# Two decoder layers on one core: expert groups of 64 and of 32 places in turn, and part of an output projection among the last heads

## The chip, the cores and the metric

The kernel runs on one core of one Trainium2 chip. The metric is the device time of that core in microseconds (us). Before the change the median of 3 runs is 1320.36 us (1319.8 to 1320.96).

## The reference, cut to what matters

256 tokens of 1024 channels pass through two layers, all in float32. The change touches the mixer of layer 0 and the mixture of experts (MoE) of both layers.

```python
# layer 0: h = x @ w_in; a convolution branch u (width 31, then LayerNorm, silu)
# beside 8 attention heads o; then one output projection of both
mix = concat([u, o], axis=-1) @ w_out + b_out          # (256, 1024) @ (1024, 1024)
x = layer_norm(ALPHA * x + mix)
# MoE of each layer: 64 experts of hidden width 256, 6 chosen for each token
def expert_step(acc, p):
    wg, wu, wd, g = p
    hid = silu(t @ wg) * (t @ wu)                      # wg, wu: (1024, 256)
    return acc + (hid @ wd) * g[:, None], None         # wd: (256, 1024)
shared = (silu(t @ sh_w_gate) * (t @ sh_w_up)) @ sh_w_down
x = layer_norm(ALPHA * x + routed + shared)
```

Layer 1 has 16 heads of another kind of attention in place of layer 0's mixer. The sum over the experts doesn't depend on the order in which they are taken, but for rounding.

## The kernel before

Five engines run programs of their own and meet at semaphores: SyncE (SP) issues nearly all large DMAs, TensorE (PE) multiplies, ScalarE (ACT) and VectorE (DVE) take results out of PSUM, GpSimd (POOL) does small work. PSUM has 8 banks; `plan_banks` lists the use of each bank in the order of the program, and an engine waits on `bank_free` or `bank_full` of a bank with the count that this list gives.

**Experts.** The 64 experts of a layer are worked off in 16 groups of 4 (`GE`). One group's weights are 12 pieces of 1 MB (gate, up and down of 4 experts) and fill 12 of the 13 units of `ring`. There is no second set: a unit is filled for the next group as soon as this group's last matmul on it is done. SP does this in `refill`, which for each piece waits on the PSUM bank of the matmuls that last use the unit (`last_use_of_weights`), and then issues the DMA. It does so in one of two orders:

```python
IN_ORDER = [(j, w) for j in range(GE) for w in range(2)] + [(j, 2) for j in range(GE)]
BY_KIND = [(j, w) for w in range(3) for j in range(GE)]
```

`j` is the expert of the group, `w` is 0 for gate, 1 for up, 2 for down. `IN_ORDER` thus brings gate and up of expert 0, then of expert 1, and so on, and all downs at the end; `BY_KIND` all gates, then all ups, then all downs. The order is that of the group that lets the units go, not of the group that the weights are for.

A group has one of two forms. The *wide* form has 64 places for the tokens of each expert. It works on pairs of experts: gate and up of experts 0 and 1 together (`gate_up(lp, 0)`, line 1016, one bank), then of experts 2 and 3, then the down products by pairs (line 1039), and last it scatters the rows back onto the tokens (line 1119). The *narrow* form has 32 places for each, so that the 4 experts stand side by side: all gates (line 1141), all ups (the same line, another bank), all downs (line 1169), scatter (line 1178). Each group also gathers the tokens of the group after it, into `xg` for a wide one (line 987) or `xn` for a narrow one (`pairs`, line 1051).

The experts stand sorted by the number of their tokens from the second half of group 0 on, the fullest first. `KINDS` says which form the groups have: 5 wide ones (`first`, three of the kind `wide`, and `turn`, which gathers for a narrow one), then 11 narrow ones. The wide groups are written out, the narrow ones are a loop of two groups a turn on PE, ACT and DVE. Between `turn` and the first narrow group stands `shared_down`, the down product of the shared expert (line 979).

**Layer 0's mixer.** The program of the heads is `attention`: scores of head h+1, then `between(h)`, then the product with V for a pair of heads (bank key `ot`, line 696), then the transposition of the probabilities (`pt`, line 705). In layer 0 `between` is `conv`, which puts parts of the convolution on PE (line 804), and DVE has its parts of the convolution (line 1564) between the softmax of the heads. After the heads PE transposes the convolution's result to rows (`urow`, line 817), DVE and ACT do LayerNorm and silu on it, and meanwhile PE begins the output projection `mix` with the attention half (its `ks` are 2 and 3, line 830): 4 results of 128x512, for each of them 4 matmuls. Then come the transpositions `uT` (line 845) and the convolution half of `mix` (`ks` 0 and 1). An fp32 matmul stands in the trace as two records, so that those 16 matmuls are x32.

## Time and profile before

| what | value |
| --- | --- |
| median of 3 runs | 1320.36 us |
| profiled execution | 1321.53 us |
| its span, first to last instruction | 1319.8 us |
| mean granted TensorE clock | 0.928 of full |
| busy: PE, DVE, ACT, POOL | 1075.3, 416.3, 259.1, 79.6 us |
| DMA | 447.53 MB, mean 339 GB/s |

The span is 1.7 us shorter than the execution's own time. The 40 slices of the page (33 us each) show five stretches: the mixer of layer 0 up to about 165 us, its experts up to about 650 us at 390 to 423 GB/s with one slice of 362, the mixer of layer 1 up to about 805 us, its experts up to about 1305 us in the same manner, and a short end. The page's chain of work that ended last has DMA and PE as its two large shares.

### The profile page before, as it was taken

To read this page: it belongs to the slowest core of one execution; us is meant where nothing else is said; L and a number is where in the kernel's file an instruction comes from. 1 tells how busy PE (TensorE), PEld (TensorE's weight loads), DVE (VectorE), ACT (ScalarE), POOL (GpSimd) and SP (SyncE) were. 2 spreads that over 40 slices of the span, in tenths; PEclk is the share of its full clock that TensorE was granted. 3 is DMA by queue.
4 is the path that set the end of the run, shared out by engine and by line. 5 is a ranking of instruction groups with operands and counts; after the bars stand their busy time and mean duration, and the time that the engine had idled before them with its cause. 6 is when DMAs were issued, how large, how long until landed. Compare 5 with 4: busy or idle time off the path is not lost.

```text
span 1319.8 us, 19934 instructions
## 1 busy us (share of the span) xinstructions
PE 1075.3 (81%) x7616; PEld 644.1 (49%) x7616; DVE 416.3 (32%) x993; ACT 259.1 (20%) x619; POOL 79.6 (6%) x106
## 2 busy tenths in 40 slices
PE   7977999999777776676499999999997777676663
PEld 4764744544444443343288866445444444333341
DVE  2584633332212222211322235333322122222113
ACT  3562322121111111111022233222211111111110
POOL 1343100000000000000141000000000000000000
PEclk9998999999988888888799999999999888888887
DMA  8172479999899999999971263699999999999994
GB/s 346 58 286 96 176 283 390 416 416 418 362 421 422 423 422 421 422 422 421 363 243 37 92 255 128 263 393 415 418 416 372 421 422 422 422 422 422 422 422 173
DMA packets 78946, 447.53 MB, mean 339 GB/s; under 512 B 7579, under 2 KB 20311, under 8 KB 29734
## 3 DMA queue, kind: packets, MB, share of 16 engines
q1 hardware_dynamic: 75840, 439.25, 81.6%
q0 software_dynamic: 1904, 6.46, 1.4%
q10 hardware_dynamic: 1142, 1.01, 0.2%
q8 instruction: 39, 0.64, 0.2%
q14 instruction: 21, 0.17, 0.0%
HBM read 445.61 MB, written 1.05 MB: 338 GB/s over the span
## 4 chain that ended last, share of the span: by engine, by line
PE 56%; DMA 35%; issue 3%; DVE 2%; SPq 2%; ACT 1%; ACTq 0%; DVEq 0%; POOL 0%; POOLq 0%
DMA ring<-in_l_exp_w_up 34%; PE bank L1016 11%; PE bank L1141 10%; PE bank L1039 5%; PE bank L866 4%; PE bank L830 4%; PE bank L987 3%; PE bank L1119 3%; PE bank L932 2%; PE bank L869 2%; PE bank L743 2%; SPq L583 2%; DMA mixT<-in_l_conv_w 1%; PE bank L979 1%; DVE side L1564 1%
## 5 line engine op out<-in xcount | busy, mean ns | idle before, releaser
L1141 PE MATMUL bank<-ring,big 128*32 128x256 f32 x2816 | 216.1, 475 | 147.5 <-DMA ring<-in_l_exp_w_up 110.2
L1141 PEld LDWEIGHTS bank<-ring,big 128*32 128x32 f32 x2816 | 120.1, 135 | 238.2 <-issue 195.0
L1016 PE MATMUL bank<-ring,big 128*64 128x512 f32 x640 | 142.2, 596 | 0.0
L1905 DVE TENSOR_TENSOR big<-big,bank 128x256 f32<-128x256 f32 x22 | 9.3, 421 | 331.8 <-PE bank L1141 331.8
L1926 DVE TENSOR_TENSOR mixT<-mixT,bank 128x512 f32<-128x512 f32 x128 | 84.1, 683 | 29.7 <-PE bank L1119 16.7
L1169 PE MATMUL bank<-ring,big 128*32 128x512 f32 x704 | 80.5, 595 | 8.6 <-DMA ring<-in_l_exp_w_down 7.3
L1411 ACT ACTIVATE ys_high<-bank,gcol 128x512 fp32r<-128x512 f32 x84 | 57.7, 687 | 147.6 <-PE bank L1169 88.2
L1016 PEld LDWEIGHTS bank<-ring,big 128*64 128x64 f32 x640 | 44.0, 137 | 82.1 <-issue 80.5
L1051 PE MATMUL bank<-pick,xs_high 128*128 128x128 f32 x352 | 82.9, 280 | 0.0
L2035 POOL TENSOR_TENSOR rstd<-rstd,half 128x1 f32<-128x1 f32 x10 | 13.3, 1333 | 1133.1 <-DVE rstd L1499 1133.1
L1051 PE MATMUL bank<-pick,xs_low 128*128 128x128 f32 x352 | 81.0, 275 | 0.0
L1039 PE MATMUL bank<-ring,big 128*64 128x512 f32 x320 | 73.1, 598 | 0.0
L1051 PEld LDWEIGHTS bank<-pick,xs_high 128*128 128x128 f32 x352 | 67.6, 192 | 9.9 <-issue 9.9
L1178 PE MATMUL bank<-ys_high,hot 128*128 128x512 f32 x88 | 42.5, 482 | 32.6 <-DVE ys_low L1913 21.8
L1051 PEld LDWEIGHTS bank<-pick,xs_low 128*128 128x128 f32 x352 | 67.5, 192 | 0.0
L866 PE MATMUL bank<-xT,ring 128*128 128x256 f32 (+1 forms) x320 | 59.8, 349 | 3.8 <-issue 3.8
L1398 ACT ACTIVATE big<-bank 128x256 f32<-128x256 f32 x44 | 16.9, 384 | 232.5 <-PE bank L1051 232.5
L1913 DVE SCALAR_TENSOR_TENSOR ys_low<-bank,gcol,ys_high 128x512 fp32r<-128x512 f32 x44 | 33.0, 751 | 83.4 <-ACT ys_high L1411 83.4
L830 PE MATMUL bank<-ring,mixT 128*128 128x512 f32 x128 | 57.5, 604 | 0.8 <-ACT mixT L1351 0.8
L866 PEld LDWEIGHTS bank<-xT,ring 128*128 128x128 f32 x320 | 53.5, 202 | 9.3 <-issue 4.3
L1178 PEld LDWEIGHTS bank<-ys_high,hot 128*128 128x128 f32 x88 | 16.4, 186 | 76.7 <-issue 58.9
L1866 DVE SCALAR_TENSOR_TENSOR ys_low<-bank,gcol,ys_high 128x512 fp32r<-128x512 f32 x40 | 30.0, 750 | 64.5 <-ACT ys_high L1411 64.5
(285 smaller groups left out, 1362.0 us busy)
## 6 DMA issues: line engine op xcount, KB each, us to landing
ring<-in_l_exp_w_gate SPq DMA_DIRECT2D x128, 1024.0 KB, 16.8
ring<-in_l_exp_w_up SPq DMA_DIRECT2D x128, 1024.0 KB, 16.9
ring<-in_l_exp_w_down SPq DMA_DIRECT2D x120, 1024.0 KB, 18.4
ring<-in_l_w_in SPq DMA_DIRECT2D x12, 1024.0 KB, 12.2
ring<-in_l_w_out SPq DMA_DIRECT2D x8, 1024.0 KB, 5.8
ring<-in_l_exp_w_down SPq DMA_DIRECT2D x16, 512.0 KB, 15.7
ring<-in_l_w_in SPq DMA_DIRECT2D x4, 1440.0 KB, 14.9
par<-in_l_ln_g POOLq DMA_DIRECT2D x4, 512.0 KB, 6.4
```

What stands on the lines that cost most here:

```text
L830: ins = mm(ps[:], mixT[:, 2 * k + j, P * tb:P * tb + P], w[:, j, HALF * h:HALF * h + HALF], start=start, stop=stop)
L866: ins = mm(ps[:, T * s + t.start:T * s + t.stop], w[:, c, P * s:P * s + P], xT[:, c, t], start=(c == 0), stop=(c == C - 1))
L987: ins = mm(ps[:, 0:GSLOT], xs[k][:, tb, P * c:P * c + P], pick[:, tb, :], start=(tb + k == 0), stop=(tb + k == 2))
L1016: ins = mm(ps[SLOTS * q:SLOTS * q + SLOTS, :], xg[:, c, SLOTS * j:SLOTS * j + SLOTS], both[:, c], start=(c == 0), stop=(c == C - 1))
L1039: ins = mm(ps[SLOTS * q:SLOTS * q + SLOTS, :], hidT[pr][:, m, SLOTS * q:SLOTS * q + SLOTS], wt[:, m, HALF * h:HALF * h + HALF], start=(m = ...
L1051: ins = mm(ps[:, n * s:n * s + n], xs[k][:, tb, P * (2 * c + s):P * (2 * c + s) + P], pick[:, tb, 0:n], start=(tb + k == 0), stop=(tb + k ...
L1119: ins = mm(ps[:], hot[:, pr, P * tb:P * tb + P], ys[k][:, pr, HALF * h:HALF * h + HALF], start=(pr + k == 0), stop=(pr + k == 2))
L1141: ins = mm(ps[r, 0:HID], xn[:, c, r], loop_weights(L, j, w)[:, c, :], start=(c == 0), stop=(c == C - 1))
L1169: ins = mm(ps[r, :], hidT[0][:, m, r], loop_weights(L, j, 2)[:, m, HALF * h:HALF * h + HALF], start=(m == 0), stop=(m == 1))
L1178: ins = mm(ps[:], hot[:, 0, P * tb:P * tb + P], ys[k][:, 0, HALF * h:HALF * h + HALF], start=(k == 0), stop=(k == 1))
L1411: fn(ys[0][:, pr, HALF * h:HALF * h + HALF], ps[:], ACT.Copy, scale=gcol[:, pr:pr + 1])\
L1926: lp.done(v.tensor_tensor(part, part, ps[:], ALU.add), ("scatter", n))
```

## The change

It has four parts.

1. The groups have the forms wide, wide, narrow, wide, narrow, wide, narrow, wide, narrow, and then 7 narrow ones: still 5 wide and 11 narrow. `PLACE` keeps the sorted experts with the form that they had: the wide groups take places 0 to 4 of the sorted list, as before. Each single group is now written out on every engine, SP too; the loop has 6 of the last 7 narrow groups. A narrow group ahead of a wide one gathers for the wide form.
2. `shared_down` stands after the ninth group in place of the fifth.
3. In layer 0's mixer PE does 4 of the attention half's 16 matmuls (first two results, `ks` 2) in `between(8)` and `between(9)`, behind the last head, and the next 4 (the same results, `ks` 3) ahead of the transpositions `urow`; the other 8 stay behind them. The banks change with it: `urow` has 0 and 1, the first two results have 6 and 7. The convolution half for the first 128 tokens waits for their `uT` alone.
4. On DVE the last piece of the convolution comes after the last head's probabilities, not before them.

```diff
-KINDS = (("first", 1), ("wide", 3), ("turn", 1), ("narrow", 11))
+KINDS = (("first", "wide", "wide", 1), ("turn0", "wide", "narrow", 1),
+         ("back0", "narrow", "wide", 1), ("turn1", "wide", "narrow", 1),
+         ("back1", "narrow", "wide", 1), ("turn2", "wide", "narrow", 1),
+         ("back2", "narrow", "wide", 1), ("turn3", "wide", "narrow", 1),
+         ("single", "narrow", "narrow", 1), ("narrow", "narrow", "narrow", 7))
+PLACE = (0, 1, 5, 2, 6, 3, 7, 4, 8, 9, 10, 11, 12, 13, 14, 15)
+ALONE = [k for k, _, _, n in KINDS if n == 1]
+LATE = TIMES["narrow"]
...
     for tb in range(TB):
-        u.add(("urow", tb), 6 + tb)
+        u.add(("urow", tb), tb)
     for tb in range(TB):
         for h in range(2):
-            u.add(("mix", 0, tb, h), 2 * tb + h)
+            u.add(("mix", 0, tb, h), [6, 7, 2, 3][2 * tb + h])
...
+    def next_place(self):
+        if self.r is None and self.kind != "narrow":
+            return GE * PLACE[BEGIN[self.kind] + 1]
+        return self.groups(GE, GE)
```

On SyncE:

```diff
-                lp = ExpertLoop(L, "wide", banks, S, bank)
-                with sp.Fori(0, dict(KINDS)["wide"]) as i:
-                    lp.i = i
-                    refill(lp, in_place(lp.groups(GE, GE)))
...
+                for kind in ALONE[1:]:
+                    lp = ExpertLoop(L, kind, banks, S, bank, i=0)
+                    refill(lp, in_place(lp.next_place()))
```

On TensorE, in layer 0's mixer (`attention`, `conv`, and behind the heads):

```diff
-                    if h < heads:
+                    if h < heads or L == 0:
                         between(h)
...
+                if h >= H0:
+                    if h == H0:
+                        for g in range(2):
+                            bank_moved(pe, ("ot", 0, g))
+                    mix(0, 0, h - H0, (2,), last=False)
+                    return
...
+            for g in range(2, H0 // 2):
+                bank_moved(pe, ("ot", 0, g))
+            for h in range(2):
+                mix(0, 0, h, (3,), first=False, last=False)
+            bank_moved(pe, "convT")
+            pe.wait_ge(S("conv_dve"), 1)
+            pe.wait_ge(S("conv_pool"), TAPS)
...
-            for g in range(H0 // 2):
-                bank_moved(pe, ("ot", 0, g))
-            for tb in range(TB):
-                for h in range(2):
-                    mix(0, tb, h, (2, 3), last=False)
+            for h in range(2):
+                mix(0, 1, h, (2, 3), last=False)
...
-                if L == 0:
-                    for tb in range(TB):
+                for tb in range(TB):
+                    if L == 0:
                         bank_moved(pe, ("uT", tb))
-                for tb in range(TB):
                     for h in range(2):
```

On TensorE, in the experts:

```diff
-                        pairs(lp, (0, 1))
+                        gathers(lp, (0, 1, 2, 3))
...
-                        pairs(lp, (2, 3))
+                        gathers(lp, (4, 5, 6, 7))
...
-                for i in range(dict(KINDS)["wide"]):
-                    wide(ExpertLoop(L, "wide", banks, S, bank, i=i))
-                wide(ExpertLoop(L, "turn", banks, S, bank, i=0))
+                for kind in ALONE[1:]:
+                    (wide if FORM[kind] == "wide" else narrow)(ExpertLoop(L, kind, banks, S, bank, i=0))
                 shared_down()
```

On VectorE, in the heads of layer 0:

```diff
-                    if between:
+                    if between and h < heads:
                         between(h)
...
+                    if between and h == heads:
+                        between(h)
```

ACT and DVE get the same choice between `gathered` and `pair` in both forms (`tokens`).

TensorE behind the last heads of layer 0, before. L705 transposes probabilities, L696 is the product with V, L817 is `urow`, L830 is `mix`, with the bank of each:

```order
L705 MATMUL bank3<-ident,att 128x128 [waits probs,bank_free3]
L705 MATMUL bank3<-ident,att 128x128 x2
L696 MATMUL bank4<-att,V 64x256 [waits bank_free3,bank_free2,bank_free4]
L696 MATMUL bank4<-att,V 64x256
L696 MATMUL bank4<-att,V 64x128 x2
L817 MATMUL bank6<-ident,side 128x128 [waits conv_pool,bank_free6,conv_dve,bank_free5]
L817 MATMUL bank6<-ident,side 128x128 x3
L817 MATMUL bank7<-ident,side 128x128 [waits bank_free7]
L817 MATMUL bank7<-ident,side 128x128 x3
L830 MATMUL bank0<-ring,mixT 128x512 [waits bank_free4,bank_free0,unit_full10]
L830 MATMUL bank0<-ring,mixT 128x512
L830 MATMUL bank0<-ring,mixT 128x512 [waits unit_full11]
```

At this place nothing of the projection stands ahead of `urow`. The same place now, where L816 is `mix`, L721 the transposition, L712 the product with V:

```order
L816 MATMUL bank6<-ring,mixT 128x512 [waits bank_free6,unit_full10,bank_free4]
L816 MATMUL bank6<-ring,mixT 128x512
L721 MATMUL bank3<-ident,att 128x128 [waits probs,bank_free3]
L721 MATMUL bank3<-ident,att 128x128 x2
L816 MATMUL bank7<-ring,mixT 128x512 [waits unit_full10,bank_free7]
L816 MATMUL bank7<-ring,mixT 128x512
L712 MATMUL bank4<-att,V 64x256 [waits bank_free3,bank_free2,bank_free4]
L712 MATMUL bank4<-att,V 64x256
L712 MATMUL bank4<-att,V 64x128 x2
L816 MATMUL bank6<-ring,mixT 128x512 [waits unit_full11,bank_free4]
L816 MATMUL bank6<-ring,mixT 128x512
L816 MATMUL bank7<-ring,mixT 128x512 [waits unit_full11]
```

Four matmuls of `mix`, into banks 6 and 7, have moved around the last transposition of probabilities, and the next four follow the last product with V (the fourth of them is cut off here), with `urow` behind them.

TensorE at the start of the third group of layer 0, before: the gate factors are transposed (L1090), then come the two products of gate and up of a wide group (L1016), each of 16 matmuls on the weights of two experts, and the transposition of the hidden rows (L1027):

```order
L1090 MATMUL bank2<-ident,att 128x128 [waits bank_free2,moe0_pick]
L1090 MATMUL bank2<-ident,att 128x128 x3
L1016 MATMUL bank0<-ring,big 64x512 [waits unit_full6,bank_free0,unit_full7,bank_free5,unit_full9,bank_free4,unit_full10,bank_free1]
L1016 MATMUL bank0<-ring,big 64x512 x15
L1016 MATMUL bank1<-ring,big 64x512 [waits unit_full3,unit_full1,unit_full4,unit_full0,bank_free1]
L1016 MATMUL bank1<-ring,big 64x512 x15
L1027 MATMUL bank0<-ident,big 128x128 [waits bank_free0]
L1027 MATMUL bank0<-ident,big 128x128
```

These wait for the gates and ups of two experts each. The same place now: the end of the second group's scatter (L1141), gate factors transposed (L1151), then all gates and all ups of a narrow group (L1163), and the gathering for the wide group after it (L1008):

```order
L1141 MATMUL bank7<-ys_high_51,hot_53 128x512
L1141 MATMUL bank7<-ys_low_52,hot_53 128x512
L1151 MATMUL bank0<-ident,att 128x128 [waits bank_free0,moe0_pick]
L1151 MATMUL bank0<-ident,att 128x128
L1163 MATMUL bank0<-ring,big 32x256 [waits unit_full9,unit_full6,unit_full0,bank_free0,unit_full3,bank_free5,bank_free4]
L1163 MATMUL bank0<-ring,big 32x256 x31
L1163 MATMUL bank1<-ring,big 32x256 [waits unit_full1,unit_full10,unit_full4,unit_full7,bank_free1]
L1163 MATMUL bank1<-ring,big 32x256 x31
L1008 MATMUL bank4<-pick_54,xs_high_49 128x256 [waits bank_free4,moe0_pick]
```

The third group's first product waits for the gates of 4 experts, and its second for the ups. In the fourth group the wide form's rows stand as before.

## Rows read from the trace of the kernel before

**Rows 1.** The page's chain that ended last, by line
```profile
DMA ring<-in_l_exp_w_up 34%; PE bank L1016 11%; PE bank L1141 10%; PE bank L1039 5%; PE bank L866 4%; PE bank L830 4%; PE bank L987 3%; PE bank L1119 3%; PE bank L932 2%; PE bank L869 2%; PE bank L743 2%; SPq L583 2%; DMA mixT<-in_l_conv_w 1%; PE bank L979 1%; DVE side L1564 1%
```

**Rows 2.** Windows: stretch, its length, busy us (instructions) by engine, PEclk, DMA share, GB/s
```profile
265.00:295.00 30.00, 30.00 (x153) 14.29 (x152) 9.36 (x18) 6.46 (x16) 0.00 (x0) 1.00 1.00 416
372.00:402.00 30.00, 20.75 (x208) 12.02 (x204) 6.30 (x12) 3.38 (x8) 0.00 (x0) 0.89 1.02 423
```

**Rows 3.** Timeline, SP: start, us, and what, each group's first weight DMA
```profile
212.34 0.35 SPq L583 DMA_DIRECT2D ring<-in_l_exp_w_gate  x1
...
242.54 0.34 SPq L583 DMA_DIRECT2D ring<-in_l_exp_w_gate  x1
...
302.92 0.34 SPq L583 DMA_DIRECT2D ring<-in_l_exp_w_gate  x1
...
337.02 3.19 SPq L583 DMA_DIRECT2D ring<-in_l_exp_w_gate  x4
...
872.97 0.35 SPq L583 DMA_DIRECT2D ring<-in_l_exp_w_gate  x1
...
997.66 2.03 SPq L583 DMA_DIRECT2D ring<-in_l_exp_w_gate  x4
```

**Rows 4.** Timeline, PE, narrow groups of layer 0: ups, gates, ups, ups
```profile
361.03 6.01 PE L1141 MATMUL bank<-ring,big 128*32 128x256 f32 x64 [4.50 <-DMA ring<-in_l_exp_w_up]
...
380.89 3.66 PE L1141 MATMUL bank<-ring,big 128*32 128x256 f32 x64 [1.63 <-DMA ring<-in_l_exp_w_gate]
390.83 6.46 PE L1141 MATMUL bank<-ring,big 128*32 128x256 f32 x64 [6.28 <-DMA ring<-in_l_exp_w_up]
...
420.63 5.23 PE L1141 MATMUL bank<-ring,big 128*32 128x256 f32 x64 [6.28 <-DMA ring<-in_l_exp_w_up]
```

**Rows 5.** Windows of 1 us around two first DMAs, columns as in Rows 2
```profile
212.00:213.00 1.00, 1.00 (x8) 0.42 (x6) 0.31 (x1) 0.38 (x1) 0.00 (x0) 1.00 0.04 16
...
336.00:337.00 1.00, 1.00 (x24) 0.76 (x20) 0.00 (x0) 0.12 (x1) 0.00 (x0) 1.00 0.00 0
```

**Rows 6.** Timeline, PE, second group: both gate and up products
```profile
205.07 13.96 PE L1016 MATMUL bank<-ring,big 128*64 128x512 f32 x64
```

**Rows 7.** Timeline behind layer 0's last heads, all engines
```profile
104.98 3.08 DVE L1564 SCALAR_TENSOR_TENSOR side<-side,cols 128x256 f32<-128x256 f32 x4
105.07 0.19 ACT L1249 ACTIVATION_READ_ACCUMULATOR att<-att,mx 128x1 f32 x1
...
105.20 0.52 PE L705 MATMUL bank<-ident,att 128*128 128x128 f32 x3
...
108.86 0.52 PE L705 MATMUL bank<-ident,att 128*128 128x128 f32 x3 [3.14 <-DVE att L1537]
...
110.05 1.55 PE L696 MATMUL bank<-att,V 128*64 128x256 f32 x8 [0.67 <-ACT att L1254]
...
111.64 0.38 ACT L1259 ACTIVATE mixT<-bank 128x256 f32<-128x256 f32 x1 [1.73 <-PE bank L696]
...
112.44 1.97 PE L817 MATMUL bank<-ident,side 128*128 128x128 f32 x8 [0.84 <-ACT side L1345]
...
114.20 15.13 PE L830 MATMUL bank<-ring,mixT 128*128 128x512 f32 x32
...
118.84 0.63 ACT L1348 ACTIVATE side<-side 128x512 f32<-128x512 f32 x1 [1.88 <-DVE side L1662]
...
129.16 1.04 PE L845 MATMUL bank<-ident,side 128*128 128x128 f32 x8
...
129.80 1.08 ACT L1351 ACTIVATE mixT<-bank 128x512 f32<-128x512 f32 x2 [10.33 <-PE bank L845]
...
130.99 4.53 PE L830 MATMUL bank<-ring,mixT 128*128 128x512 f32 x10 [0.79 <-ACT mixT L1351]
```

**Rows 8.** Windows of 2 us, PE alone: stretch, length, busy us, PEclk, DMA share, GB/s
```profile
104.00:106.00 2.00, 1.58 (x13) 1.00 0.30 45
...
112.00:114.00 2.00, 1.56 (x8) 0.50 0.98 322
```

More of the change, by code:

```diff
@@ L233, in __init__ @@
         self.tag = f"{'moe' if r is None else 'more'}{L}"
-        self.slots = NSLOT if kind == "narrow" else SLOTS
+        self.form, self.after = FORM[kind], AFTER[kind]
     def here(self, per, more):
@@ L788, in prog_tensor, with mix @@
                         bank_moved(pe, (name, tb, g))
+            def mix(L, tb, h, ks, first=True, last=True):
+                key = ("mix", L, tb, h)
+                ps = bank_open(pe, key) if first else bank[banks.at[key][0]]
+                for k in ks:
+                    unit_wait(pe, (f"out{L}", k))
+                    w = by_pair(unit((f"out{L}", k)))
+                    for j in range(2):
+                        start, stop = first and (k, j) == (ks[0], 0), last and (k, j) == (ks[-1], 1)
+                        ins = mm(ps[:], mixT[:, 2 * k + j, P * tb:P * tb + P],
+                                 w[:, j, HALF * h:HALF * h + HALF], start=start, stop=stop)
+                if last:
+                    bank_made(ins, key)
             def conv(h):
@@ L1412, in high, with tokens @@
                         .then_inc(lp.own("high"), 1)
+                def tokens(lp, c):
+                    if lp.after == "wide":
+                        gathered(lp.read, lp.done, ("gather", c))
+                    elif c % 4 == 0:
+                        pair(lp, c // 2)
                 def wide(lp):
@@ L1847, in wide @@
                 def wide(lp):
-                    after = "narrow" if lp.kind == "turn" else "wide"
                     if lp.kind == "first":
@@ L1949, in prog_vector @@
                 more = dve.value_load(rounds[0:1, 0:1], min_val=0, max_val=MAXR - 1)
[L1950 to L1952 removed]
+                for kind in ALONE[1:]:
+                    (wide if FORM[kind] == "wide" else narrow)(ExpertLoop(L, kind, banks, S, bank, i=0))
                 for tb in range(TB):
```

154 lines of the change are left out of this document (69 added, 85 removed).

## The prediction, made before the changed kernel ran

> **What bounds the kernel now.** I read first the page's chain by line, to see who carries the end [rows 1]: DMA of expert weights has 34%, and next to it stand PE lines of the wide groups (1016, 1039) and of the mixers (866, 830). So there are two regimes, and the windows by stage separate them [rows 2]. Among the wide groups PE is busy 30.00 of 30 us; among the narrow ones 20.75 of 30, and the DMA share is full in both, 416 and 423 GB/s. The experts are thus near a tie in the wide form and bound by DMA in the narrow one. How near is read from SP's first weight DMA of each group [rows 3]: 242.54 - 212.34 = 30.20 us for a wide group. For a narrow group the start of the ups repeats after 390.83 - 361.03 = 29.80 and 420.63 - 390.83 = 29.80 us [rows 4]; So 12 pieces take 29.80 us, 2.483 us a piece. That is what the weights need, whatever PE does.
>
> The rest is where DMA stands still inside the experts. In the window 212 to 213 it moves 16 GB/s, in 336 to 337 nothing [rows 5]: each time the ring is full and the first unit not yet let go. The second place is the change of form. From 302.92 to 337.02 are 34.10 us, 4.30 over 29.80 [rows 3]: the last wide group's 30.2 us and `shared_down` lie ahead of the first narrow gates.
>
> In the mixer I read the timeline behind the last heads [rows 7]: PE has nothing from 105.72 to 108.86, then works at half clock, and from 114.20 on is the bound with the projection until the transpositions `uT` at 129.16.
>
> **The experts, step by step.** Group 0 and group 1 stay wide, so group 2's first DMA still comes at the 212.34 of the trace, less what the mixer gives. To the first DMA of group 6 (337.02) the kernel takes 124.68 us for four groups, and 4 x 29.80 = 119.20 would do: 5.48 us to be had. In layer 1 it is 997.66 - 872.97 = 124.69, so 5.49 [rows 3]. The later groups are at 29.8 already. Whether the new order gets all of it depends on each group letting its first unit go within 29.80 us of its own weights' first issue, I. Two steps:
>
> Wide behind narrow. The narrow group refills by kind, so the wide group's first product (experts 0 and 1) needs the sixth piece. From issue to use there is a lag: 361.03 - 337.02 = 24.01 us for eight pieces, which take 19.87, so 4.14 [rows 3, 4]. Start: I + 4.14 + 6 x 2.483 = I + 19.04. PE has waited then, and is cold. The product takes 13.96 / 2 = 6.98 warm [rows 6]; the cold start costs 6.46 - 3.66 = 2.80 at most and 5.23 - 3.66 = 1.57 at least, by the narrow ups that also follow a wait for DMA [rows 4]. End I + 28.8, and SP issues 0.3 later (205.07 + 6.98 = 212.05 against 212.34 [rows 3, 6]): I + 29.1. It is 0.7 us in time, 1.9 with the small penalty. This is the tightest place of the change, three times a layer.
>
> Narrow behind wide. The wide group then ends its 30.2 us at I + 19.04 + 30.20 + 2.80 = I + 52.0, that is 22.2 after the narrow weights' first issue; the gates (seventh piece, at 4.14 + 17.38 = 21.5) are there. Gates 3.66 [rows 4], so the first unit goes at 26.2: 3.6 us in time. The four other products of that group have the wide gather's eight pieces beside them, about 1 us of waits for banks 0 and 1; PE reaches the next wide group some 6 us before its sixth piece, which hides it.
>
> The moved `shared_down` costs 6.9 us of PE (16 records; its slot is in the 34.10) and now stands where PE is idle 9 us of 30 [rows 2]. The next gates end at about 24 after issue, inside 29.8. Cost 0; without the cover it would be its 6.9 a layer. The written-out code adds instructions to every engine, no work to any: as many wide and narrow groups as before. The wide groups, written out already, run with PE 30.00 of 30 busy [rows 2], so I cost it at 0.
>
> Sum of the experts: 5.48 + 5.49 = 11.0 us.
>
> **The mixer, step by step** [rows 7]. Before, the last transposition waits for DVE (3.14 us), which does its 3.08 us of convolution first. Now the probabilities start when ACT has the exponentials, 105.26, and are there by 106.1 (the 0.8 between 108.06 and 108.86). PE goes on at 105.72 with two matmuls of `mix` at 0.86 (4 records at 13.8 / 32 = 0.43, warm): 107.44. Transposition to 107.96; two more matmuls beside ACT's copy of it: 109.7. Product with V, 1.55 at the low clock, some 0.8 warm: 110.6 with the waits at either end. ACT's copy of it, 0.38: 111.0. Four matmuls, 3.44: 114.45. Then `urow`; the convolution is in time: DVE ends at about 106.2 + 3.1 = 109.3, POOL before. `urow` takes 1.04 warm (the eight of 129.16), then eight matmuls, 6.88: 122.4. The silu of the second half ends 119.47 - 112.44 = 7.03 after `urow` starts, at 121.5: 0.9 in time. So `uT` starts at 122.4 in place of 129.16, 6.8 us. The first convolution half no longer waits for ACT's second copy: 1.08 / 2 = 0.54.
>
> Clock: 1.00 at 104 to 106, 0.50 at 112 to 114 behind the idle 3 us [rows 8]. Full is 2.4 GHz and 0.50 is 1.2 GHz. Now PE has no such gap. If it fell all the same, product, `urow` and the first matmuls would be as slow as now, 0.7 + 0.9 + 0.6 = 2.2 us less. Ends of this part: 5.1 and 7.4; I take 7.2, near the warm one, since what lowered the clock is filled. What follows (LayerNorm, router, group 0) keeps its distances, so the whole comes earlier by it.
>
> **Sum.** 11.0 + 7.2 = 18.2 us. The profiled execution of 1321.53 becomes 1303.3; it lies 1.2 above the median, and from 1320.36 the forecast is 1302.2.
>
> **Against it.** In the narrow stage the clock is down when PE comes back from DMA: 64 records take 6.01, 6.46 and 5.23 us instead of 3.66 [rows 4]. The Trainium skill, TensorE: Matmul & The Clock Gate, section "HAM oscillation — how this bites in real kernels", says that a kernel whose matmul pieces each follow a wait for DMA pays for the cold clock at every piece. The trace agrees for these rows; it shows too that the penalty ends inside the piece. The change puts the wide product behind such a wait. That is the rival on the other side.
>
> **Rivals.** (a) Cold wide groups: the first wide product runs at 1.2 GHz to its end, 13.96 instead of 9.8. It ends at I + 33.0, the next DMA comes at 33.3, 3.5 late; six times 21 us. 18.2 - 21 leaves the kernel at 1323, slower. It decides once the penalty passes 3.5 us. Against it: no ups row costs over 2.80. 4%. (b) The tight place is missed a little, 0.5 to 1 us each, or the first narrow gates come late: 3 to 6 us of the gain go, 1305.2 to 1308.2. For it: only 0.7 us of slack. 14%. (c) The mixer gives little, because PE's inserted matmuls hold the last head back or LayerNorm becomes the wait: 0 to 3 us, 1306.4 to 1309.4. Against it: the slack worked out above. 5%. (d) The DMA stream doesn't close up, since something I don't see holds SP (it now loads the experts' numbers in straight code): only the mixer's 7.2, 1313.2. 4%. (e) Both parts give nothing, the order only moves the waits: 1320, 3%. The forecast, 1300.5 to 1304.8, has 70%.
>
> **How the numbers follow.** A difference of 0.2% (2.6 us) is what a measurement here can tell. Faster: 70 + 14 + 5 + 4 = 93%. Same: 3%. Slower: 4%. The range 1300.0 to 1308.0 takes the forecast, (b) nearly whole and a third of (c).
>
> **What would show it.** SP's first weight DMAs from group 2 to group 6 stand 29.8 apart, with no window under 400 GB/s between 215 and 630 us (less the 7); `uT` at about 122; the wide L1037 product behind a wait for DMA, under 10 us for its first half, PE idle in the wide groups and not DMA. A penalty over 3.5 us, gaps of SP over 30 us, or `uT` later than 124 would prove a step wrong.

## The result, and the profile after

The changed kernel takes 1303.57 us (median of 4 runs, 1301.92 to 1303.92), the kernel before on the same chip 1320.66 us (1319.8 to 1322.14, 4 runs). The ratio is 0.9857, with an interval of 0.9839 to 0.9876: 1.4% faster, 17.1 us by the medians. The forecast was 1302.2 in 1300.0 to 1308.0.

The profiled execution of the changed kernel took 1301.92 us with a span of 1300.2, at a mean clock of 0.931. It is the fastest of its four, and the profiled execution before was above its median, so the two profiles differ by 19.6 us where the medians differ by 17.1. Landmarks on PE cut both spans into the same stretches; each is the start of a named product, and each distance is taken inside one profile:

| from, to | before | after | gain | forecast |
| --- | --- | --- | --- | --- |
| start to group 1's first product, layer 0 | 205.07 | 197.61 | 7.46 | 7.2 |
| to the last group's ups, layer 0 | 425.11 | 420.19 | 4.92 | 5.48 |
| to the first transposition of layer 1 | 24.61 | 24.48 | 0.13 | 0 |
| to layer 1's first projection product | 5.94 | 2.68 | 3.26 | 0 |
| to group 1's first product, layer 1 | 204.96 | 204.79 | 0.17 | 0 |
| to the last group's ups, layer 1 | 424.13 | 420.34 | 3.79 | 5.49 |
| to the end | 29.95 | 30.07 | -0.12 | 0 |

The page's chain for the kernel after, by engine and by line, to be set beside [rows 1]:

```profile
PE 52%; DMA 39%; issue 3%; DVE 2%; SPq 2%; ACT 1%; ACTq 0%; DVEq 0%; POOL 0%; POOLq 0%
DMA ring<-in_l_exp_w_up 33%; PE bank L1037 12%; PE bank L1163 10%; DMA ring<-in_l_exp_w_gate 5%; PE bank L888 5%; PE bank L816 4%; PE bank L1060 3%; PE bank L953 2%; PE bank L891 2%; PE bank L759 2%; PE bank L1141 2%; SPq L604 2%; PE bank L1008 1%; PE bank L1072 1%; DMA mixT<-in_l_conv_w 1%
```

DMA now has 39% of the chain (35% before), of which `ring<-in_l_exp_w_up` has 33%, about as before, and the gates have a share of their own (5%): the waits for weights have spread. PE is still the larger half (56% before, 52% now).

The windows of the kernel after, one of 30 us for each of four groups in turn and the ones behind (columns as in [rows 2]):

```profile
216.00:246.00 30.00, 28.32 (x262) 18.02 (x260) 11.61 (x22) 6.87 (x15) 0.00 (x0) 1.00 1.01 420
246.00:276.00 30.00, 24.27 (x110) 10.05 (x112) 5.54 (x11) 4.02 (x11) 0.00 (x0) 0.89 1.02 422
276.00:306.00 30.00, 27.67 (x255) 17.70 (x252) 11.89 (x22) 5.91 (x13) 0.00 (x0) 1.00 1.01 421
306.00:336.00 30.00, 23.25 (x103) 9.23 (x101) 3.61 (x8) 4.02 (x11) 0.00 (x0) 0.83 1.01 420
...
449.00:479.00 30.00, 21.59 (x208) 11.87 (x208) 6.30 (x12) 3.38 (x8) 0.00 (x0) 0.83 1.02 422
```

Where PE had 30.00 of 30 us in wide groups it now has idle time in every window, and DMA has none: 420 to 422 GB/s in each. Of the two hollow spots of [rows 5] the one at the change of form is gone. The one behind group 1's first product stays, since the change doesn't touch that group, and both kernels pay for it; it is the first window below. The other three are the same point in the turns, 3 us around each first DMA that a wide group lets go:

```profile
204.00:207.00 3.00, 3.00 (x16) 1.01 (x14) 0.42 (x1) 0.38 (x1) 0.00 (x0) 1.00 0.37 87
...
262.00:265.00 3.00, 3.00 (x17) 1.08 (x15) 0.42 (x1) 0.38 (x1) 0.00 (x0) 1.00 1.02 423
...
322.00:325.00 3.00, 3.00 (x16) 1.09 (x14) 0.42 (x1) 0.38 (x1) 0.00 (x0) 1.00 1.04 431
...
381.00:384.00 3.00, 3.00 (x18) 1.09 (x16) 0.42 (x1) 0.38 (x1) 0.00 (x0) 1.00 1.04 434
```

SP's first weight DMA of groups in the timeline after, answering to [rows 3]:

```profile
204.89 0.36 SPq L604 DMA_DIRECT2D ring<-in_l_exp_w_gate  x1
...
262.77 0.34 SPq L604 DMA_DIRECT2D ring<-in_l_exp_w_gate  x1
...
289.77 1.89 SPq L604 DMA_DIRECT2D ring<-in_l_exp_w_gate  x4
...
323.29 0.34 SPq L604 DMA_DIRECT2D ring<-in_l_exp_w_gate  x1
...
382.11 0.34 SPq L604 DMA_DIRECT2D ring<-in_l_exp_w_gate  x1
...
412.08 1.90 SPq L604 DMA_DIRECT2D ring<-in_l_exp_w_gate  x4
```

A stream with no hole would have these at 204.89 plus multiples of 29.80: 264.49, 294.29, 324.09, 383.69, 413.49 for the ones shown. Each issue is ahead of its due time, by 1.7, 4.5, 0.8, 1.6 and 1.4 us. The first, third and fourth are let go by wide groups, for which the prediction worked out 0.7 to 1.9; the second by a narrow group, for which it had 3.6. The last is that of the ninth group, which starts late itself (below).

PE in the same stretch: a narrow group's gates and ups, the wide pair that begins behind a wait for DMA, and the ninth group's gates and ups:

```profile
228.06 7.11 PE L1163 MATMUL bank<-ring,big 128*32 128x256 f32 x128 [0.72 <-issue]
...
253.46 16.00 PE L1037 MATMUL bank<-ring,big 128*64 128x512 f32 x64 [5.51 <-DMA ring<-in_l_exp_w_up]
...
406.52 8.80 PE L1163 MATMUL bank<-ring,big 128*32 128x256 f32 x128 [1.99 <-DMA ring<-in_l_exp_w_gate]
```

The wide pair starts at 253.46, where I + 19.04 from the due issue 234.69 gives 253.73 (I is the issue of a group's own first weights, as in the prediction). It takes 16.00 us instead of 13.96 [rows 6]; the two others (at 313.06 and 372.67, so 59.60 and 59.61 apart, twice 29.80) show 16.92 and 16.1. The granted clock is 0.50 in the window of 251 to 257, 0.95 in 257 to 263 and 1.00 behind it. So the cold start costs 2.0 to 3.0 us a pair.

Behind layer 0's heads, PE in the timeline after, answering to [rows 7]:

```profile
105.35 0.52 PE L721 MATMUL bank<-ident,att 128*128 128x128 f32 x3
...
105.70 1.88 PE L816 MATMUL bank<-ring,mixT 128*128 128x512 f32 x4
...
107.42 0.49 PE L721 MATMUL bank<-ident,att 128*128 128x128 f32 x3
...
107.75 1.88 PE L816 MATMUL bank<-ring,mixT 128*128 128x512 f32 x4
...
109.56 0.87 PE L712 MATMUL bank<-att,V 128*64 128x256 f32 x8
...
110.96 3.67 PE L816 MATMUL bank<-ring,mixT 128*128 128x512 f32 x8 [0.53 <-ACT mixT L1280]
...
114.47 1.04 PE L858 MATMUL bank<-ident,side 128*128 128x128 f32 x8
...
115.35 7.03 PE L816 MATMUL bank<-ring,mixT 128*128 128x512 f32 x16
...
123.50 14.00 PE L816 MATMUL bank<-ring,mixT 128*128 128x512 f32 x32 [0.25 <-ACT mixT L1372]
```

The window after that answers to [rows 8]:

```profile
112.00:114.00 2.00, 2.00 (x6) 1.00 0.92 279
```

No wait is over 0.8 us, and the window of 112 to 114 has the full clock (2.4 GHz) where [rows 8] had half of it. `uT` follows at 122.22. Counted from the last transposition but one, it comes after 16.87 us instead of 23.96: 7.09 us, free of what differs ahead of it. The convolution half of `mix` then starts 1.28 us after `uT` instead of 1.83, another 0.55.

### The profile page after: what moved, and what is told of

Read it like the earlier page. It is cut to its first block, busy times and chain, and to the rows that moved or that the text cites. A ratio compares the mean times of both kernels' runs of the same rounds, so it can differ in the third digit from the quotient of the medians.

```text
span 1300.2 us, 19603 instructions
## 1 busy us (share of the span) xinstructions
PE 1069.3 (82%) x7616; PEld 643.1 (49%) x7616; DVE 417.1 (32%) x993; ACT 259.7 (20%) x619; POOL 79.9 (6%) x106
## 4 chain that ended last, share of the span: by engine, by line
PE 52%; DMA 39%; issue 3%; DVE 2%; SPq 2%; ACT 1%; ACTq 0%; DVEq 0%; POOL 0%; POOLq 0%
DMA ring<-in_l_exp_w_up 33%; PE bank L1037 12%; PE bank L1163 10%; DMA ring<-in_l_exp_w_gate 5%; PE bank L888 5%; PE bank L816 4%; PE bank L1060 3%; PE bank L953 2%; PE bank L891 2%; PE bank L759 2%; PE bank L1141 2%; SPq L604 2%; PE bank L1008 1%; PE bank L1072 1%; DMA mixT<-in_l_conv_w 1%
## 5 line engine op out<-in xcount | busy, mean ns | idle before, releaser
L1163 PE MATMUL bank<-ring,big 128*32 128x256 f32 x2816 | 191.6, 435 | 99.9 <-DMA ring<-in_l_exp_w_up 70.5
L1163 PEld LDWEIGHTS bank<-ring,big 128*32 128x32 f32 x2816 | 114.3, 124 | 171.8 <-issue 131.0
L1037 PE MATMUL bank<-ring,big 128*64 128x512 f32 x640 | 156.2, 643 | 37.4 <-DMA ring<-in_l_exp_w_up 37.4
L1037 PEld LDWEIGHTS bank<-ring,big 128*64 128x64 f32 x640 | 50.0, 148 | 127.9 <-issue 126.3
L1191 PE MATMUL bank<-ring,big 128*32 128x512 f32 x704 | 85.3, 625 | 12.5 <-DMA ring<-in_l_exp_w_down 11.5
L1950 DVE TENSOR_TENSOR mixT<-mixT,bank 128x512 f32<-128x512 f32 x128 | 84.6, 683 | 29.2 <-PE bank L1141 16.9
L1929 DVE TENSOR_TENSOR big<-big,bank 128x256 f32<-128x256 f32 x22 | 9.3, 421 | 255.7 <-PE bank L1163 255.7
L1060 PE MATMUL bank<-ring,big 128*64 128x512 f32 x320 | 73.1, 598 | 0.0
L1882 DVE TENSOR_TENSOR big<-big,bank 128x256 f32<-128x256 f32 x20 | 8.4, 421 | 162.8 <-ACT big L1424 162.8
L816 PE MATMUL bank<-ring,mixT 128*128 128x512 f32 x128 | 56.9, 595 | 0.8 <-ACT mixT L1280 0.5
```

The costliest lines, as they stand in the source:

```text
L816: ins = mm(ps[:], mixT[:, 2 * k + j, P * tb:P * tb + P], w[:, j, HALF * h:HALF * h + HALF], start=start, stop=stop)
L1037: ins = mm(ps[SLOTS * q:SLOTS * q + SLOTS, :], xg[:, c, SLOTS * j:SLOTS * j + SLOTS], both[:, c], start=(c == 0), stop=(c == C - 1))
L1060: ins = mm(ps[SLOTS * q:SLOTS * q + SLOTS, :], hidT[pr][:, m, SLOTS * q:SLOTS * q + SLOTS], wt[:, m, HALF * h:HALF * h + HALF], start=(m = ...
L1163: ins = mm(ps[r, 0:HID], xn[:, c, r], loop_weights(L, j, w)[:, c, :], start=(c == 0), stop=(c == C - 1))
L1191: ins = mm(ps[r, :], hidT[0][:, m, r], loop_weights(L, j, 2)[:, m, HALF * h:HALF * h + HALF], start=(m == 0), stop=(m == 1))
L1950: lp.done(v.tensor_tensor(part, part, ps[:], ALU.add), ("scatter", n))
```

## The experiments

All times are medians. Each kernel ran beside the kernel before on one chip, and its ratio, with the 95% interval, is to that; the first row stands for the two parts alone, five wide first and shared_down at the seam (beside the others the kernel before had 1321.38 and 1321.85). "d" is the time from group 1's first product to the last group's ups, in layer 0 and layer 1. A stream without a hole gives 7.27 + 13 x 29.80 + 24.0 = 418.7: 7.27 to group 1's first issue, 13 groups, and [rows 3, 4]'s 24.01 from issue to ups.

| kernel | us (runs) | ratio | d, layer 0 / 1 | layer 1's start |
| --- | --- | --- | --- | --- |
| before | 1321.49 (13) | | 425.1 / 424.1 | 5.94 |
| mixer alone | 1313.5 (10) | 0.995 [0.9933, 0.9968] | 424.1 / 424.1 | 6.12 |
| groups alone | 1309.84 (4) | 0.9912 [0.9889, 0.9936] | 420.2 / 420.2 | 2.68 |
| five wide first, rest as after | 1309.48 (4) | 0.9912 [0.9888, 0.9936] | 421.8 / 421.9 | 2.68 |
| same, 11 narrow of the looped kind | 1314.0 (4) | 0.9941 [0.9924, 0.9958] | 424.7 / 424.1 | 6.02 |
| turns, shared_down at the seam | 1305.34 (4) | 0.988 [0.9856, 0.9905] | 421.5 / 421.1 | 2.68 |
| turns, refill by pairs | 1302.4 (4) | 0.9854 [0.9835, 0.9873] | 420.5 / 420.3 | 2.68 |
| wide pair waits for eight pieces | 1325.45 (6) | 1.0033 [1.002, 1.0046] | 429.5 / 430.0 | 2.67 |
| no swap on VectorE | 1304.02 (4) | 0.9873 [0.9857, 0.989] | 420.7 / 420.2 | 2.68 |

### The two parts apart

The first kernel is the one before with the mixer's edits (TensorE's `mix` pieces among the heads, banks, the order on VectorE), its expert code untouched. Against the changed kernel its core is:

```diff
-KINDS = (("first", "wide", "wide", 1), ("turn0", "wide", "narrow", 1),
...
+KINDS = (("first", 1), ("wide", 3), ("turn", 1), ("narrow", 11))
```

The second is the changed kernel with the mixer of before:

```diff
-                mix(0, 0, h, (3,), first=False, last=False)
...
-            for h in range(2):
-                mix(0, 1, h, (2, 3), last=False)
+            for tb in range(TB):
+                for h in range(2):
+                    mix(0, tb, h, (2, 3), last=False)
```

> The kernel before with the change to layer 0's mixer alone (parts 3 and 4). Theory: the mixer's 7.4 us (uT 129.16 -> 122.22, and the first convolution half 0.5 earlier) come through to the end whole, since all that follows only starts earlier: 1320.7 - 7.4 = 1313.3, and SyncE's first weight DMA of group 2 of layer 0 comes at 204.9 in place of 212.34, with the 34.1 us step at the change of form still there. Rival: the gain is given back later (LayerNorm or the early weights become the wait): over 1316.

> The changed kernel with the mixer of before (parts 1 and 2 alone). Theory: 4.9 us from the experts of layer 0 and 3.8 from those of layer 1, as between the two traces, so 1320.7 - 8.7 = 1312.0, and a further 3.3 us less only if the wait of 3.79 us at the start of layer 1 (which the changed kernel's trace does not have) goes by the change of the expert code. Rival: the two parts share a gain: over 1315.

The mixer alone gives 0.5%: 6.6 us (4.2 to 8.9). `uT` is at 121.60, and d and layer 1's start are those of the old order. Its d in layer 0 is 424.1, where the profile before has 425.1; the kernel before with 64 unused instructions (below) has 424.3. So some 0.9 us of the 425.1 belong to that one execution. The groups alone give 0.88%, 11.6 us (8.5 to 14.7). Their sum, 18.2, is that of the whole within the intervals, which are some 5 us wide: no interplay of the two parts is seen. Of the groups' 11.6 their profile has 4.9 and 3.9 in d and 3.3 at the start of layer 1, which the prediction had not foreseen.

### Turns, or the place of shared_down?

The prediction gave all of the 5.48 us a layer to the new order, and nothing to the place of `shared_down`. Two kernels separate them. One keeps the new place and the written-out code, and puts the five wide groups first; the other keeps the turns and puts `shared_down` back behind the last wide group.

```diff
-         ("back0", "narrow", "wide", 1), ("turn1", "wide", "narrow", 1),
...
+KINDS = (("first", "wide", "wide", 1), ("wide1", "wide", "wide", 1),
+         ("wide2", "wide", "wide", 1), ("wide3", "wide", "wide", 1),
+         ("turn0", "wide", "narrow", 1), ("single0", "narrow", "narrow", 1),
+         ("single1", "narrow", "narrow", 1), ("single2", "narrow", "narrow", 1),
...
+PLACE = tuple(range(16))
```

> The changed kernel with its five wide groups first again (wide x5, then narrow x11), all else kept: mixer, shared_down behind the ninth group, groups written out. Theory: most of the experts' gain is shared_down leaving the seam between the last wide and the first narrow group, since without its 6.9 us the first gates let their units go about 27 us after the issue, within 29.8; what turns add is only the 0.4 us that each of three further wide groups is over 29.8. So within 0 to 1.2 us a layer of the changed kernel: 1303.6 to 1306. Rival: the turns are what closes the stream: 4 to 5 us a layer slower, 1312 to 1313.

```diff
+                    if kind == "single":
+                        shared_down()
...
-                shared_down()
```

> The changed kernel with shared_down between the eighth (wide) and the ninth (narrow) group, so ahead of a narrow group's gates that a wide group has already made late. Theory: the gates end about 22.2 + 1 + 6.9 + 3.7 = 33.8 us after the issue in place of 26.9, 4.3 over 29.8 as before the change, so some 4 us a layer: 1311 to 1312, with SyncE's first DMA for the tenth group over 33 us after its slot before. Rival: the groups in turn have made slack for it: the same as the changed kernel within 1 us.

Five wide first: d is 421.8 and 421.9. Shared at the seam: 421.5 and 421.1. So either part alone closes more than half of the gap that both close. Neither expectation was met: the first kernel loses 1.6 us a layer to the changed one, more than the 1.2 that its theory allowed and less than half of its rival's 4 to 5; the second loses 1.3 and 0.8, nearer to its rival (the same within 1 us) than to the 4 a layer of its theory. By time the first is behind the changed kernel (0.9888 to 0.9936 against 0.9839 to 0.9876); the second isn't told apart from it.

Why the seam costs so little in turns is seen in PE's timeline of that kernel:

```profile
402.28 7.03 PE L1000 MATMUL bank<-ring,side 128*128 128x512 f32 x16
409.14 0.38 PE L1151 MATMUL bank<-ident,att 128*128 128x128 f32 x2
410.24 7.11 PE L1163 MATMUL bank<-ring,big 128*32 128x256 f32 x128 [0.72 <-issue]
```

The 7 us of `shared_down` lie ahead of gates that would otherwise wait for DMA until about 404; they start at 410.24 and let the first unit go at 414.11 (SP's next issue), 1.8 us after the 412.3 that its stream asks for. In the old order all of it came on top of wide groups that held PE 30.2 us each, longer than their weights took. In turns the last wide group itself starts behind a wait for DMA, so PE isn't behind when it reaches the seam.

### The old order in the new code

One more kernel completes the square: the five-wide-first kernel, with 11 narrow groups of the looped kind, so that `shared_down` is back behind the fifth group.

```diff
-         ("turn0", "wide", "narrow", 1), ("single0", "narrow", "narrow", 1),
-         ("single1", "narrow", "narrow", 1), ("single2", "narrow", "narrow", 1),
-         ("single", "narrow", "narrow", 1), ("narrow", "narrow", "narrow", 7))
+         ("turn0", "wide", "narrow", 1), ("narrow", "narrow", "narrow", 11))
```

> The experts as in the five-wide-first kernel, with its mixer, but all 11 narrow groups are of the looped kind (10 in five turns of the loop and the last by itself), as in the kernel before, where the five-wide-first kernel has 4 of them written out and 6 in three turns. shared_down stands right behind the fifth group again. At stake: the 3.3 us at the start of layer 1 (5.94, 6.12 and 5.85 us from the first transposition to the first projection with the old expert code, 2.68 in all eight profiles with the new). Theory A, they hang on how much of the narrow groups is looped: 5.9 here. Theory B, they hang on something else that the new expert code brought, such as wide groups and SP's part written out: 2.68 here. Expert stage of layer 0, first product of the second group to the last ups: 421.8 if written-out narrow groups cost and give nothing and the place of shared_down is free; up to 425.1 if the old place of shared_down is what costs. Time 1307 to 1313 us.

Here d is 424.7 and 424.1, as before the change, and the time, 1314.0, that of the mixer alone (1313.5): within these measurements the wide groups and SP's part written out cost and give nothing. SP's first issue at the seam, in the timeline of this kernel:

```profile
331.15 3.01 SPq L602 DMA_DIRECT2D ring<-in_l_exp_w_gate  x4
```

The same in the five-wide-first kernel:

```profile
324.91 1.90 SPq L604 DMA_DIRECT2D ring<-in_l_exp_w_gate  x4
```

Counted from group 1's first product (199.22 and 200.07) these are 131.93 and 124.84, 7.1 us apart: that is `shared_down`'s 7.03. The stream needs 7.27 + 4 x 29.80 = 126.5. With it the seam is 5.5 us late, without it 1.6 early. By the profiles the two kernels differ by 8.0 us of span (2.8, 2.1 and 3.3 of them in d and at layer 1's start), by their medians only by 4.5: the five-wide-first kernel's profiled execution, 1305.41, is the fastest of its four. The square in layer 0: 424.7 (old order, old place), 421.8 (new place), 421.5 (turns), 420.2 (both).

These two kernels differ in one more thing: four narrow groups are written out in one, none in the other. Splitting d at the ups of the seventh group keeps the seam apart from what follows. Up to there the five-wide-first kernel is ahead by 4.3 us in layer 0 and 3.7 in layer 1. In the nine groups behind, where no release is late in either, it gives some of that back: 270.1 and 270.0 us against 268.7 and 268.4 with the looped groups (268.4 to 268.5 in the mixer alone and the kernel before with 64 unused instructions). PE's timeline of the five-wide-first kernel, ups of the eighth to the eleventh group:

```profile
381.63 5.95 PE L1163 MATMUL bank<-ring,big 128*32 128x256 f32 x64 [4.60 <-DMA ring<-in_l_exp_w_up]
...
412.37 5.95 PE L1163 MATMUL bank<-ring,big 128*32 128x256 f32 x64 [7.19 <-DMA ring<-in_l_exp_w_up]
...
442.22 3.66 PE L1163 MATMUL bank<-ring,big 128*32 128x256 f32 x64 [0.52 <-DMA ring<-in_l_exp_w_up]
...
472.66 6.51 PE L1163 MATMUL bank<-ring,big 128*32 128x256 f32 x64 [5.14 <-DMA ring<-in_l_exp_w_up]
```

Two of the three distances, 30.74 and 30.44, are over 29.80. So the seam is worth some 4 us a layer, and the 2.9 of the square is what is left of it once the groups behind have lost 1.4 to 1.6. No run separates whether they lose it by being written out or by the moved `shared_down`; the changed kernel loses a like amount at its ninth group, ahead of `shared_down`.

### How tight is the tight place

The first wide product behind a narrow group is made to wait for all eight gate and up pieces, not for four of them, in three groups a layer.

```diff
-                        for q in range(2):
+                        late = pr == 0 and lp.kind in ("turn1", "turn2", "turn3")
+                        for q in range(4 if late else 2):
```

> The changed kernel, but the first product of the three wide groups behind a narrow one waits for all eight gate and up pieces: 5.0 us later than now. Theory: the slack there is 0.6 to 1.5 us (first DMA of the next group 323.29 against a due 323.9, 262.77 against 264.3), so the stream stands still 3.5 to 4.4 us at each: six times, 21 to 26 us, 1325 to 1330, slower than the kernel before. Rival: the stream has slack elsewhere (the ring's later units): under 10 us.

SP's first issues of two such groups in the timeline:

```profile
272.32 0.34 SPq L604 DMA_DIRECT2D ring<-in_l_exp_w_gate  x1
...
334.84 0.35 SPq L604 DMA_DIRECT2D ring<-in_l_exp_w_gate  x1
```

The windows of 4 us ahead of the first of them and around it:

```profile
266.00:270.00 4.00, 4.00 (x16) 1.30 (x14) 0.00 (x0) 0.00 (x0) 0.00 (x0) 0.76 0.97 406
270.00:274.00 4.00, 4.00 (x20) 1.39 (x18) 0.42 (x1) 0.38 (x1) 0.00 (x0) 1.00 0.20 49
```

The hole is back (49 GB/s), the issues are 62.5 apart instead of 59.6, d grows by 9.3 and 9.6 us, some 3.1 us for each of six places, and the kernel is slower than the one before the change. The product may start only two pieces (4.97 us) later. Against the full stream's 418.7 the two d are 10.8 and 11.3 over, 3.6 to 3.8 a place; so 1.2 to 1.4 of the 4.97 had been slack, which agrees with the 1.7, 0.8 and 1.6 read from SP above. This is the mechanism of rival (a), reached by a late start instead of a slow clock: past the slack every further us is paid in full. The pairs now begin behind 10.3 to 10.6 us without work and take 15.67 to 16.88 us: the cold start costs no more than behind 5.5.

The opposite, more slack there: a narrow group ahead of a wide one refills by pairs, so that the wide product needs four pieces, not six.

```diff
-                    for j, w in pieces or (BY_KIND if lp.form == "narrow" else IN_ORDER):
+                    for j, w in pieces or (BY_KIND if lp.form == "narrow" and lp.after == "narrow" else IN_ORDER):
```

> The changed kernel, but a narrow group in front of a wide one refills in the wide group's order (gate and up of experts 0 and 1 first), so that the wide group's first product needs four pieces and not six. Theory: it starts 5 us earlier and nearly warm (under 7.5 us), the unit is let go 5 to 7 us earlier, but the DMA stream was full already, so the time stays within 1 us of the changed kernel. Rival: the 1.5 us a layer by which the last ups come later than 29.8 us a group lie at the tight place: 2 to 3 us faster.

PE's timeline at the first wide group in turn:

```profile
247.43 7.09 PE L1037 MATMUL bank<-ring,big 128*64 128x512 f32 x32 [0.68 <-DMA ring<-in_l_exp_w_up]
257.37 4.92 PE L1037 MATMUL bank<-ring,big 128*64 128x512 f32 x14 [2.85 <-DMA ring<-in_l_exp_w_up]
```

Counted from group 1's product (196.41 here, 197.61 in the changed kernel) the first half of the pair starts 4.8 us earlier, two pieces' time; the second waits for its own pieces. SP's next issue, at 254.69, comes 6.9 us earlier. Nothing is gained (1302.4 to 1303.57, intervals over each other; d 420.5 and 420.3): where the stream has no hole, an earlier release buys nothing. It would only be an insurance.

### The order on VectorE

The changed kernel with the last piece of the convolution ahead of the last probabilities, as before.

```diff
-                    if between and h < heads:
+                    if between:
```

> The changed kernel with VectorE's last convolution piece ahead of the last head's probabilities again (part 4 undone). Theory: TensorE does its four matmuls while it waits, the last transposition stands at 108.9 in place of 107.4, product with V 110.0 in place of 109.56, so only 0.5 to 1 us is lost: within 1 us of the changed kernel. Rival: the swap carries the mixer's gain (the chain over the probabilities bounds it): 2 us or more slower.

PE's timeline behind the last heads of that kernel:

```profile
105.14 0.52 PE L721 MATMUL bank<-ident,att 128*128 128x128 f32 x3
...
105.50 1.88 PE L816 MATMUL bank<-ring,mixT 128*128 128x512 f32 x4
...
108.81 0.52 PE L721 MATMUL bank<-ident,att 128*128 128x128 f32 x3 [1.43 <-DVE att L1560]
...
109.16 1.88 PE L816 MATMUL bank<-ring,mixT 128*128 128x512 f32 x4
```

PE waits 1.43 us, and `uT` comes 18.48 us after the last transposition but one, not 16.87: the swap on VectorE is worth 1.6 of the mixer's 7.1, the filling of the wait with products the other 5.5. The granted clock stays at 1.00 from 104 to 118 here too. In the whole time 1.6 us isn't told apart (1304.02 against 1303.57).

### The start of layer 1

In the kernel before, PE stands 3.79 us between the transpositions at the start of layer 1 and the first projection; after the change 0.52. PE's timeline of before:

```profile
654.79 1.95 PE L658 MATMUL bank<-ident,xrow 128*128 128x128 f32 x8 [6.68 <-issue]
656.66 0.28 PE L853 MATMUL bank<-ident,rows 16*128 16x16 f32 x1
660.73 4.63 PE L866 MATMUL bank<-xT,ring 128*128 128x128 f32 x20 [3.79 <-issue]
```

The same place after:

```profile
642.28 1.94 PE L674 MATMUL bank<-ident,xrow 128*128 128x128 f32 x8 [6.67 <-issue]
644.16 0.28 PE L875 MATMUL bank<-ident,rows 16*128 16x16 f32 x1
644.96 9.86 PE L888 MATMUL bank<-xT,ring 128*128 128x128 f32 x64 [0.52 <-issue]
```

No engine's work and no transfer that the profile shows ends this wait, and no edit touches the place. One theory was that PE waits for its program, and that the place of the code in memory decides how long. In four kernels (the one before, and three times the changed one) PE's program is longer by 64, or by 64, 128 and 192 empty instructions; they stand at the end of layer 0's experts in a branch that isn't taken, so that only the place of what follows moves.

```diff
+                    for _ in range(64 if L == 0 else 0):
+                        pe.nop()
```

> The kernel before with 64 empty instructions more in TensorE's program, in the branch for further rounds of layer 0, which is not taken: no work is added, only the code behind it lies further on. Theory: TensorE's wait between the first transpositions of layer 1 and its first projection (5.94 us from start to start in the kernel before and 6.12 in the mixer alone, 2.68 in every kernel with the new expert code) is a wait for code, set by where the code lies; moved, it falls to about 2.7: some 3 us faster, 1318. Rival: it belongs to the two-group loop's length or to data (LayerNorm, the projection's weights): 5.9 stays, and the time too.

> The changed kernel with the same 64 unused instructions. Theory of the code's place: the 2.68 us stay, or become about 6 if this place is an unlucky one; at least one of the three shifts (64, 128, 192) should differ from the others somewhere at the start of layer 1 if the place decides. Rival: all three stay at 2.68.

> As the run with 64, with 128 unused instructions: about 2.7 or about 6 us between the first transpositions of layer 1 and its first projection, by the place of the code; 2.68 in all three if it isn't the place.

> As the run with 64, with 192 unused instructions: about 2.7 or about 6 us by the place of the code; 2.68 in all three if it isn't the place.

The theory fell. The kernel before with 64 more has 5.85 us (and 0.9996 [0.9985, 1.0007] in time), the three others 2.68 each; in one execution each they took 1299.48, 1305.88 and 1303.64 us. Their d is 420.2 in layer 0 in all three, and what moves the sum is the start, group 1's first product at 196.43, 201.77 and 199.50: executions of programs that are the same up to there differ by 5 us in the first 200. That also tells how far the 7.46 of one pair of profiles is to be trusted.

The old order in the new code gave the other clue. With its 11 narrow groups of the looped kind the gap is 6.02 us, as PE's timeline of that kernel shows:

```profile
649.45 0.28 PE L873 MATMUL bank<-ident,rows 16*128 16x16 f32 x1
653.59 6.58 PE L886 MATMUL bank<-xT,ring 128*128 128x128 f32 x37 [3.86 <-issue]
```

With four of them written out and six in the loop (five wide first) it is 2.68. The place of `shared_down` differs between these two as well, but the kernel that has the turns and `shared_down` at the seam has 2.68 too. So the 3.3 us go with how the narrow groups are coded, not with the turns. By what mechanism, whether through the turns of the loop or through the length of the code behind the fifth group, no run tells; the shifts tried stop at 192 instructions.

## Why the prediction was right

**The mixer.** Forecast 7.2 us with ends 5.1 and 7.4. Up to `uT` that was 6.8 us, and the distance inside the profile shrank by 7.09; the 0.54 of the convolution half came as 0.55. `uT` was forecast at 122.4 and came at 122.22. The clock stayed up, as the larger end assumed. By time the part alone gave 6.6 (4.2 to 8.9).

**The tight place.** The start I + 19.04 held within 0.3 us (253.46 against 253.73). The penalty of the cold start was forecast as 1.57 to 2.80 and was 2.0 to 3.0; the slack left 0.8 to 1.7, with 0.7 to 1.9 forecast. The Trainium skill's rule for pieces that each wait for DMA ("TensorE: Matmul & The Clock Gate", section "HAM oscillation — how this bites in real kernels") holds here as far as a penalty appears at each of them; the wide pair's 16.0 to 16.9 us show that it stays bounded, and [rows 3]'s successors that the slack pays for it. Rival (a) needed 3.5 us and got 3.0.

**The experts' sum** was 11.0 and came out at 8.7. The term that fails is the full stream behind the turns: d is 420.2 and 420.3 where 418.7 was due, so 1.5 and 1.6 us a layer are missing. "The later groups are at 29.8 already" was itself not quite so: in layer 0 of the profile before, the last two groups took 30.24 and 30.13 us, which is most of the 0.9 us that this profile has over other executions of the old order. Against those, layer 0 gains 4.0 us and not 4.9, and the experts 7.8.

In layer 0 nearly all of the 1.5 appears at one place, the ninth group. Its gates should start at 383.69 + 4.14 + 17.38 = 405.2 and start at 406.52, and the groups behind keep that distance (438.81 for the next ups, where 413.49 + 24.01 = 437.5 was due, and 617.80, which is six times 29.83 later). Five other profiles with the turns and the new place of `shared_down` show the same 1.3 to 1.4 us there (the one without the swap 2.0); in layer 1 it comes at the eighth or the ninth group. SP is in time (412.08 for 413.49), so it isn't a late release. Nor is it the stream's rate: between the wide pair's start at 372.67 and the gates at 406.52 lie 13 pieces of 1024 KB, 13.63 MB, and the queue of the weights moved 14.18 MB in that time. The 0.55 MB too much are worth the 1.3 us, so bytes that these gates didn't need went ahead of some that they did; why, no view tells. It goes with the narrow groups that are written out: the kernels with all 11 of the looped kind don't have it. That is where "costed at 0" is in doubt, and the cause stays open.

**shared_down.** "Cost 0" at its new place held. What failed is the attribution: I gave the 5.48 us to the order of the groups, while the place of `shared_down` alone brings 2.9 in layer 0 and 2.1 in layer 1, the turns alone 3.2 and 3.0, both 4.5 and 3.7 (against the old order in the new code). They overlap; the likely reason is that each takes PE off the critical path at the same seam. The prediction had read that seam rightly, as the wide group's 30.2 us and `shared_down` ahead of the narrow gates, and then credited its 4.30 us to the turns alone. That both parts were in the change is why the attribution did no harm to the number.

**Written-out code** was costed at 0. For the wide groups and SP this held. For the narrow ones it was wrong by a gain of 3.26 us at the start of layer 1. This and the 2.3 us missing in the experts have opposite signs: that the sum of 18.2 stands between the medians' 17.1 and the profiles' 19.6 is in part luck, since two errors offset each other. Without the unforeseen 3.26 us the time would be about 1306.8 by the median, 4.6 off the forecast and still inside the range.

**The rivals.** (d) and (e) are excluded by the windows, (c) by `uT`. (b) named 3 to 6 us and late releases; 2.3 to 3.2 us are missing in the experts, but no release was late.

## What to carry to other kernels

Where stages bound by the engine and stages bound by a transfer follow one another, and the buffer is released in small units, mixing them lets the slack of one pay for the excess of the other; but work out for each turn how long before its due time the first unit goes, since past that point every us is lost at each turn (six starts held back by 5 us each cost 19 us in the experts' stretches, 22 by the medians). Look for fixed work at the seam first: moving a 7 us product off it brought some 60% of what it brought together with the reordering. And compare distances inside each profile, since executions of programs alike up to that point differed by 5 us before the changed part began.

## What the runs showed of the hardware

- A pair of products of 13.96 us that begins behind 5.4 to 6.8 us without work takes 15.93 to 16.92 us, 2.0 to 3.0 more and not twice its time; the windows of the wide groups in turn have a granted clock of 0.83 to 0.89, and it is back at 1.00 before the pair ends. Behind 10.3 to 10.6 us without work the pair takes 15.67 to 16.88 us, so the longer wait costs no more.
- With products put into a wait of 3 us on TensorE the granted clock stays at 1.00, even where 1.43 us of the wait are left, and more than their own time comes back: 5.5 us for 8 records of `mix` moved ahead (3.76 us). Without them it fell to 0.50 behind the wait [rows 8].
- TensorE stood 3.3 us longer at the start of layer 1 where all narrow groups ahead of it were of the looped kind. 64 unused instructions more left the wait there, and 64 to 192 more didn't bring it back where it was gone. The cause is open.
- A weight can be 1.3 us late at its use although its DMA was issued in time and the queue moved 420 GB/s all along: 14.18 MB had passed where the pieces up to it hold 13.63.
